# Splitting the last three even output tiles into latent and context parts, with the odd norm between them

## The reference, cut to what matters

```python
def second_block(...):
    for i in range(DEPTH):                      # i = 0 even, i = 1 odd
        h_lat = rms_norm_2(x_lat, norm_g[i]) * (1.0 + sc_l) + sh_l
        h_ctx = rms_norm_2(x_ctx, norm_g[i]) * (1.0 + sc_c) + sh_c
        y_lat, y_ctx = even_mixer(...) if i % 2 == 0 else odd_mixer(...)
        x_lat = x_lat + g_l * y_lat             # y = mixed @ w_out
        if update_ctx:                          # true for i = 0 alone
            x_ctx = x_ctx + g_c * y_ctx
    return rms_norm_2(x_lat, final_g)

def odd_mixer(h_lat, h_ctx, w_in, ...):
    cv, cgl, cg, dq, dk, dv, dg = split_cols(h_lat @ w_in, ODD_WIDTHS)
    oc = conformer_conv(cv, cgl, cg, dw_w, dw_b, ln_g, ln_b)   # 31 taps along the rows
```

## Time and profile before

| | us |
|---|---|
| median of three runs | 2627.19 (2627.0 to 2627.4) |
| the profiled execution: its own time | 2626.77 |
| its span, first to last instruction | 2625.00 |
| TensorE busy | 2535.7 (97%) |
| VectorE busy | 1646.6 (63%) |
| ScalarE busy | 1124.7 (43%) |
| mean granted TensorE clock | 0.992 |

### The profile page before, as it was taken

How to read it: one execution, slowest core, us unless ns; L and a number is a source line. 1 busy time by engine, 2 the same in 40 slices (tenths; PEclk the granted TensorE clock), 3 DMA queues, 4 the chain that set the end, 5 groups by cost and what they waited for, 6 DMA issues and landing times.

```text
span 2625.0 us, 34953 instructions
## 1 busy us (share of the span) xinstructions
PE 2535.7 (97%) x13470; PEld 2049.4 (78%) x13470; DVE 1646.6 (63%) x3123; ACT 1124.7 (43%) x2043; POOL 0.2 (0%) x4
## 2 busy tenths in 40 slices
PE   8999999999999999999999999999999999999998
PEld 6878888678888878788886788888876666888666
DVE  6766555455446776665653644478486677499764
ACT  4336443543222243464434422233345667232563
POOL 0000000000000000000000000000000000000000
PEclk9999999999999999999999999999999999999999
DMA  4220033123336522201331233375110000232311
GB/s 159 92 69 22 17 121 124 37 73 105 96 97 214 187 74 91 66 16 38 124 113 41 80 97 97 96 256 180 41 49 19 23 17 17 65 87 65 84 48 48
DMA packets 74083, 219.38 MB, mean 84 GB/s; under 512 B 21312, under 2 KB 21568, under 8 KB 73152
## 3 DMA queue, kind: packets, MB, share of 16 engines
q1 hardware_dynamic: 48384, 176.29, 20.7%
q10 hardware_dynamic: 25536, 40.87, 5.0%
HBM read 215.03 MB, written 2.10 MB: 83 GB/s over the span
## 4 chain that ended last, share of the span: by engine, by line
PE 87%; DVE 7%; ACT 3%; issue 2%; ACTq 0%; DVEq 0%
PE bank L579 21%; PE bank L580 21%; PE bank L581 21%; PE bank L832 4%; PE bank L796 3%; PE bank L806 3%; PE bank L1401 1%; DVE w_lo L545 1%; PE bank L1388 1%; PE bank L698 1%; PE bank L610 1%; PE bank L611 1%; PE bank L612 1%; DVE e_s L897 1%; ACT w_hi L538 1%
## 5 line engine op out<-in xcount | busy, mean ns | idle before, releaser
L579 PE MATMUL bank<-a_hi,w_hi 128*128 128x512 f32 (+1 forms) x1480 | 588.9, 398 | 19.8 <-DVE w_lo L545 14.4
L538 ACT ACTIVATE w_hi<-w_raw 128x1024 fp32r<-128x1024 f32 x334 | 353.0, 1060 | 570.0 <-PE bank L581 540.9
L581 PE MATMUL bank<-a_hi,w_lo 128*128 128x512 f32 (+1 forms) x1480 | 579.1, 391 | 0.0
L580 PE MATMUL bank<-a_lo,w_hi 128*128 128x512 f32 (+1 forms) x1480 | 578.5, 391 | 0.0
L545 DVE TENSOR_TENSOR w_lo<-w_raw,w_hi 128x1024 fp32r<-128x1024 f32 x334 | 407.6, 1223 | 250.0 <-ACT w_hi L538 249.1
L579 PEld LDWEIGHTS bank<-a_hi,w_hi 128*128 128x128 f32 (+1 forms) x1480 | 277.8, 188 | 88.8 <-issue 14.4
L581 PEld LDWEIGHTS bank<-a_hi,w_lo 128*128 128x128 f32 (+1 forms) x1480 | 277.5, 188 | 60.7
L580 PEld LDWEIGHTS bank<-a_lo,w_hi 128*128 128x128 f32 (+1 forms) x1480 | 278.1, 188 | 58.3 <-issue 1.4
L579 PE MATMUL bank<-b_hi,w_hi 128*128 128x512 f32 x704 | 257.1, 365 | 1.0 <-DVE w_lo L545 0.8
L580 PE MATMUL bank<-b_lo,w_hi 128*128 128x512 f32 x704 | 248.7, 353 | 0.0
L581 PE MATMUL bank<-b_hi,w_lo 128*128 128x512 f32 x704 | 247.4, 351 | 0.0
(11 more groups left out here) (392 smaller groups left out, 3955.3 us busy)
## 6 DMA issues: line engine op xcount, KB each, us to landing
w_raw<-w_tiles SPq DMA_DIRECT2D x334, 512.0 KB, 3.5
mod_raw<-mod_tiles ACTq DMA_DIRECT2D x48, 512.0 KB, 4.2
d_bias<-rpb_rows ACTq DMA_DIRECT2D x16, 224.0 KB, 4.3
hT<-xT ACTq DMA_DIRECT2D x8, 256.0 KB, 6.1
m_in<-memT ACTq DMA_DIRECT2D x2, 1024.0 KB, 4.7
mod_cond<-cond_rows ACTq DMA_DIRECT2D x2, 1024.0 KB, 5.4
out<-hT ACTq DMA_DIRECT2D x8, 256.0 KB, 2.2
ctx_sq<-ctxT ACTq DMA_DIRECT2D x1, 1024.0 KB, 9.1
```

The source lines that it names most:

```text
L538: act.activation(w_hi[:, t % SPLIT, :], w_raw[:, t % RAW, :], ACT.Copy).then_inc(sem("w_rounded"), 1)
L579: pe.matmul(o, wh, hi[:, k, :n], start=k == 0, stop=False)
L580: pe.matmul(o, wh, lo[:, k, :n], start=False, stop=False)
L581: mm = pe.matmul(o, wl, hi[:, k, :n], start=False, stop=k == kc - 1)
```

## The change

From even output tile T5 (`EVEN_SPLIT`) on, the products are made in two passes. TensorE first makes the latent parts of T5, T6 and T7, then the context parts of T5, T6 and T7; the latent sum of squares stands after chunk 6 of the context part of T5, the latent rows after chunk 2 of that of T6. The context sum moves behind the pair T8/T9, the context rows behind T10. The three filler groups of this seam (four matmuls) are gone. VectorE and ScalarE make the odd input from the latent stream while the context parts are still being multiplied, and take the remaining three context parts between the chunks. The weight buffers of T5 to T7 come free only with their context parts.

```diff
         def even_out_pe(pe):
             group_tiles_pe(pe, [(0, 0), (0, 1)], both("e_y"), inputs_ready(("e_mix",)))
-            for c in range(2, KC):
+            for c in range(2, EVEN_SPLIT):
                 product(pe, (0, c), both("e_y"))
+            first = blocks[0] // KC
+            lat, ctx_part = both("e_y")
+            for c in range(EVEN_SPLIT, KC):
+                for _ in part_steps(pe, first + c - EVEN_SPLIT, (0, c), lat):
+                    pass
+            for c in range(EVEN_SPLIT, KC):
+                for k, _ in enumerate(part_steps(pe, first + c - EVEN_SPLIT, (0, c), ctx_part, last=True)):
+                    if c == EVEN_SPLIT and k == KC - 2:
+                        ssq_pe(pe, ("m2", 1, "lat"), S)
+                    if c == EVEN_SPLIT + 1 and k == 2:
+                        rstd_pe(pe, ("m2", 1, "lat"), S)
+        EVEN_SPLIT = KC - SPLIT
+        def part_steps(pe, t, key, part, last=False):
+            name, hi, lo, n = part
+            o = claim(pe, name, *key, hold=True)[:, :n]
+            pe.wait_ge(sem("w_split"), t + 1)
+            for k in range(KC):
+                wh, wl = head(w_hi[:, t % SPLIT, :], k), head(w_lo[:, t % SPLIT, :], k)
+                pe.matmul(o, wh, hi[:, k, :n], start=k == 0, stop=False)
+                pe.matmul(o, wh, lo[:, k, :n], start=False, stop=False)
+                mm = pe.matmul(o, wl, hi[:, k, :n], start=False, stop=k == KC - 1)
...
+                yield
...
+        def odd_begin_dve(dve):
+            lat = PARTS[0]
+            even_out_take_dve(dve, "ctx", EVEN_SPLIT)
+            lo_after(dve, "e_y/lat", 0, EVEN_SPLIT)
             for c in range(KC):
+                mod_scaled_dve(dve, 1, lat, c)
                 if c:
+                    mod_low_dve(dve, 1, lat, c - 1)
+                if c == 1:
+                    even_out_take_dve(dve, "ctx", EVEN_SPLIT + 1)
+                    lo_after(dve, "e_y/lat", 0, EVEN_SPLIT + 1)
+                if c == 2:
+                    odd_ctx_sum_dve(dve, EVEN_SPLIT)
+                if c == 4:
+                    even_out_take_dve(dve, "ctx", KC - 1)
+                    odd_ctx_sum_dve(dve, EVEN_SPLIT + 1)
+            mod_low_dve(dve, 1, lat, KC - 1)
+            odd_ctx_sum_dve(dve, KC - 1)
+            lo_after(dve, "e_y/lat", 0, KC - 1)
...
         def odd_in_pe(pe):
             group_pe(pe, [((1,), both(name)[0]) for name, *_ in OJ[:2]], mod_ready(1, "lat"))
             for i, (name, _, _, with_ctx) in enumerate(OJ):
                 if name[:2] not in LATE and i >= 2:
                     product(...)
+                if i == 1:
+                    ctx_ssq_pe(pe, 1)
+                if i == 2:
+                    ctx_rstd_pe(pe, 1)
...
             even_out_pe(pe)
-            warm_pe(pe, 2, "m2", 1)
-            ssq_pe(pe, ("m2", 1, "lat"), S)
-            ctx_ssq_pe(pe, 1)
-            warm_pe(pe, 1, "m2_rstd", 1)
-            rstd_pe(pe, ("m2", 1, "lat"), S)
-            ctx_rstd_pe(pe, 1)
-            warm_pe(pe, 1, "odd_in")
             odd_in_pe(pe)
...
             even_out_dve(dve)
-            inverse_dve(dve, ("m2", 1, "lat"), S)
+            odd_begin_dve(dve)
             ctx_inverse_dve(dve, 1)
-            lo_after(dve, "e_y/lat", 0, KC - 1)
-            mod_chunks_dve(dve, 1, PARTS[0])
             mod_chunks_dve(dve, 1, PARTS[1], 0, 2)
             for name, *_ in OJ[:2]:
                 lo_after(dve, f"{name}/lat", 1)
             mod_chunks_dve(dve, 1, PARTS[1], 2)
```

More of the change, by code:

```diff
@@ L1865, in mod_chunks_dve, with mod_scaled_dve, mod_low_dve @@
         def mod_chunks_dve(dve, i, part, first=0, last=KC):
-            p, _, sl, n, w = part
-            t = mod_tmp(i)
-            row = bank(dve, "rstd", "m2", i, p)
             for c in range(first, last + 1):
                 if c < last:
[L1872 to L1878, removed]
-                if c > first:
[L1880 to L1884, removed]
+                    mod_scaled_dve(dve, i, part, c)
+                if c > first:
+                    mod_low_dve(dve, i, part, c - 1)
+        def mod_scaled_dve(dve, i, part, c):
+            p, _, sl, n, w = part
+            row = bank(dve, "rstd", "m2", i, p)
+            if c >= 2:
+                dve.wait_ge(*when("shifted_in", i, p, c - 2))
+            dve.scalar_tensor_tensor(out=mod_tmp(i)[:, c % 2, sl], in0=stream(p)[:, c, :n],
+                                     scalar=mod_gain[:, w, c:c + 1], in1=row[:, :n], op0=ALU.mult, op1=ALU.mult)\
+               .then_inc(*(freed("rstd", "m2", i, p, also=("scaled", i, p, c)) if c == KC - 1
+                           else done("scaled", i, p, c)))
+        def mod_low_dve(dve, i, part, c):
+            p, _, sl, n, w = part
+            dve.wait_ge(*when("hi", i, p, c))
+            dve.scalar_tensor_tensor(out=b_lo[:, c, sl], in0=mod_tmp(i)[:, c % 2, sl], scalar=mod[:, i, c, w:w + 1],
+                                     in1=b_hi[:, c, sl].bitcast(f32), op0=ALU.add, op1=ALU.subtract)\
+               .then_inc(*done("shifted_in", i, p, c))
         def both(name):
@@ L2137, in even_out_pe @@
             group_tiles_pe(pe, [(0, 0), (0, 1)], both("e_y"), inputs_ready(("e_mix",)))
-            for c in range(2, KC):
+            for c in range(2, EVEN_SPLIT):
                 product(pe, (0, c), both("e_y"))
-        def even_out_dve(dve):
-            for c in range(KC):
[L2144 to L2151, removed]
-                if c:
-                    odd_sum_dve(dve, c - 1)
-            odd_sum_dve(dve, KC - 1)
@@ L2162, in odd_squares_act, with odd_square_act @@
+        def odd_square_act(act, p, c):
+            act.wait_ge(*when("h2", p, c))
+            if p == "lat":
                 if c >= 2:
@@ L2164, in odd_squares_act @@
                 act.activation(sq[:, c % 2, :], hT[:, c, :], ACT.Square).then_inc(*done("sq", "m2", 1, "lat", c))
-                act.wait_ge(*when("h2", "ctx", c))
+            else:
                 if c >= 2:
```

58 lines of the change are left out of this document (48 added, 10 removed).

## The result

| | before | changed |
|---|---|---|
| median of 20 timed runs each, us | 2627.29 (2623.34 to 2631.68) | 2630.07 (2627.49 to 2632.6) |
| the profiled execution: its own time | 2626.77 | 2629.22 |
| its span | 2625.0 | 2627.4 |
| TensorE busy | 2535.7 | 2534.5 |
| mean granted clock | 0.992 | 0.990 |

The forecast was 2629.0. The chain that ended last has the same shares as in the earlier trace rows, TensorE 87%.

What follows compares the result with a forecast made beforehand. TensorE holds 87% of the chain, but VectorE's first tap decides: T10 comes 6.15 us sooner, yet late context rows put the tap 1.84 later. 2626.77 + 1.84 = 2628.6, on the median 2629.0; range 2625.8 to 2632.3.

Steps and rivals of the forecast that it cites:

- The quantity that decides: VectorE never pauses from first tap to softmax, so the first tap's shift, +1.84 us, goes through to the end.
- Even output, sum and rows: At T5 to T7: latent sum meets TensorE without a wait; even output ends and pair starts near 2288.3, 7.3 us earlier.
- The pair: T8/T9: TensorE waits of 0.2, 0.7, then 0.1 each; end at 2300.3, T10 at 2300.75, 6.15 us ahead.
- R and the wait of VectorE: Context rows readable at 2306.9, VectorE idle from about 2301.6; first tap R + 12.65 = 2319.55, 1.84 us later.
- TensorE's two waits: 4.1 us before T11, 4.3 before T13, shrinking to 1.3 with half clock; no cost beyond the 1.84.
- T11 then takes up to 3.0 us more: Half clock expected behind the 4.1 us wait; T12 ends at 2324.7 and the loss falls into the second wait.
- Rival B: Full clock through T11's wait, half clock in T13: T16 4.1 us later, end 2631.3, or 2633.8; chance 0.12.
- They no longer cover anything: The seam's four fillers, about 3.8 us, go because the wait they stood in is gone.
- Moved DMAs: Loads of T11 to T13 hang on splits of T8 to T10, wanted seven or more us later; no cost.
- buffers (D): Bank or weight buffer held until the context parts, delaying the pair 3 us or more: 2632; chance 0.08.
- an early R (C): Context rows sooner through VectorE gaps or a shorter chain: shift -1.5 to +0.8, 2626 to 2628; chance 0.18.
- the gain arriving (A): VectorE slack before T13, or context rows before T10 ends, keeps the seam's 5.7 us: 2621.5; chance 0.06.

Runs made afterwards that it cites:

- early: Changed kernel with last context take and sums sooner, context rows inside T10, T11/T12 splits ahead of context chunks; ratio 0.9991, timed again 0.9989.
- splits first: Changed kernel with the splits of T11 and T12 ahead of the context chunks on VectorE and ScalarE; ratio 1.0005.
- the second comparison of the changed kernel: Changed kernel unaltered, profiled and timed again against the kernel before; ratio 1.0017, +4.5 us (2.1 to 6.8).
- without fillers: Kernel before with only its four filler matmuls at the seam taken out; ratio 1.0013.
- rows moved: Kernel before with only the context sum put behind the pair T8/T9 and the context rows behind T10; ratio 1.0034.
- fillers in the waits: Changed kernel with four filler matmuls behind the context rows and three ahead of T13; ratio 1.0014.
- inside T10: Changed kernel with the context rows behind chunk 1 of T10 in place of behind all of T10; ratio 0.9999.
- still later: Changed kernel with four filler matmuls in front of the context rows, behind T10; ratio 1.0023.

## Why the prediction was right, step by step

**The quantity that decides.** The prediction said that VectorE's first tap decides and that its shift goes through. In thirteen profiles softmax moved with the first tap to within 0.2 us, over a range of 12.7 us (52.90 to 65.61). For the end of the program one correction is needed. From T16 to the attention TensorE takes 91.80 to 91.85 us in all thirteen, and the timed differences go with that start: every interval in the table holds the shift of the attention column, those of early and of splits first included. The timing alone could hardly tell the two columns apart, since only the second comparison of the changed kernel leaves out the tap's shift (1.89, interval from 2.1); it is the profiles that show the difference. From the tap to T16 lie 24.57 or 24.58 us where T13 runs at full clock (the kernel before twice, without fillers, rows moved, and fillers in the waits), 25.0 to 25.2 where some 3 us of T13 run at half clock, and 26.28 where nearly 6 do. So T13's clock is part of the price: 0.45 us in the changed kernel.

**Even output, sum and rows.** Forecast pair start 2288.3, measured 2287.08 + 0.98 = 2288.06 on the clock of before. The sum does meet TensorE without a wait.

**The pair.** Forecast waits of 0.2, 0.7 and some 0.1, measured one of 0.38; end forecast 2300.3, measured 2300.24; T10 2300.75 against 2300.60.

**R and the wait of VectorE.** Forecast 2306.9 behind an idle time of 5.3 us; measured 2306.77 and 5.54. First tap forecast +1.84, measured +1.88, +1.89 and +1.86. This term carries the forecast, and the experiments that moved only the rows (inside T10, still later, moved alone) show that it is the cause and not a companion.

**TensorE's two waits.** In front of T11 4.1 forecast, 3.81 measured. In front of T13 1.3 forecast, 2.78 measured: the step "T11 then takes up to 3.0 us more" took the 6.0 us stretch of the earlier trace rows for the half clock; it lasted about 3 us and lost half as much. In the second profile there was none, and the wait was 4.40, near the 4.3 that the prediction has for full clock. That the first drop is paid out of the second wait was right; the 6.8 us of half clock in the kernel with only the rows moved cost nothing at T16 either. T16 was forecast 1.84 us later and came 2.33 later: the step that no drop costs anything beyond the tap's shift holds for T11, not for T13.

**Rival B** happened in its mechanism: T13 begins at half clock in all three profiles of the changed kernel (its first matmul takes 0.77 us for 0.47), in the second one exactly as the rival had it, with full clock in T11. Its price was wrong. It assumed 6 us of half clock (3.0 lost, 0.7 regained, T16 +4.1); about 3 us came, T16 moved by 2.33, and of that only 0.45 is the clock's. The argument that kept its chance low, that the longer waits were the ones followed by half clock, does not fit the prediction's own rows: 2.18 us was followed by it, 2.28 was not.

**The fillers.** "They no longer cover anything" holds for the changed kernel. What the prediction had no term for is what they did before: 3.6 us at the first tap (56.54 to 60.13). It cost the forecast nothing, since the context matmuls took over; as the prediction did not reckon with that, this was luck. Whoever takes fillers out without putting work there pays it.

**Moved DMAs, buffers (D), an early R (C), the gain arriving (A).** The pair waits only 0.38 us, for `b_lo` and not for a buffer. VectorE did stand at the rows. The gain was at the seam and did not arrive.

**Small slips.** The terms for the last latent part add up to 2280.13, not 2280.25, and T16's first matmul stands at 2341.51 in the trace of before, not at 2341.41. Neither bears on the sum.

**The size.** Predicted +1.8, timed +3.4 (1.8 to 5.0), so the forecast lies at the near end of the interval. T13's clock accounts for 0.45. For the rest there is one candidate with rows. Behind the attention's start TensorE waits 2.28 us for `rstd` in every profile, about 74 us in. In some executions half clock follows, in others not. Here the two profiles of the early kernel, the same code, first and second:

```profile
2501.63 2.10 PE L797 MATMUL bank<-d_k,d_q 64*128 64x512 f32 x8 [2.28 <-ACT rstd L2424]
2503.66 0.79 PE L579 MATMUL bank<-b_hi,w_hi 128*128 128x512 f32 x1
```

```profile
2505.11 1.56 PE L797 MATMUL bank<-d_k,d_q 64*128 64x512 f32 x8 [2.28 <-ACT rstd L2424]
2506.60 0.50 PE L579 MATMUL bank<-b_hi,w_hi 128*128 128x512 f32 x1
```

The mean rest of the program is 192.9 us in the seven profiles with that drop and 191.5 in the six without. The drop was in one of four profiles of the kernels with whole tiles, and in six of nine of those with split tiles; the changed kernel had it in two of three, the early one in one of two. So it is not a fixed property of a kernel. Whether a kernel's phase shifts the odds (6 of 9 against 1 of 4, times 1.4 us, would be 0.6 of the missing 1.1), these few profiles can't settle; it stays open. The spread of single executions is too large for it: the code ahead of the take is the same in both kernels, yet the take lies at 2258.91 to 2262.81 in the three profiles of the changed one. A fixed cost of the split tiles elsewhere does not show: the early kernel has them too, and its timed -2.4 and -2.9 match its attention start, 3.0 sooner, though within intervals of about 2.4 to either side.

## What to carry to other kernels

Before closing a gap of the busiest engine, find the engine that hands it work afterwards and ask which of its instructions the moved work feeds: here two small matmuls, moved behind three products on TensorE, cost VectorE 9 us, more than the closed gap gave. In a queue that runs in order, put what waits for a late result behind what could run, and the producer of that result as early as its input allows. Take fillers out only where useful work comes into their place, and see from the granted clock that it does.

## What the runs showed of the hardware

- Half clock behind identical waits is not the same from one execution to the next. Behind 3.81 us of waiting the changed kernel had some 3 us of it in one profile and none in another; with only the rows moved it was 6.8 us behind the same 3.81; behind 2.28 us, seven of thirteen profiles had some 3 us. In front of T13 the eight profiles with a wait of 2.55 to 5.72 us all had it; the five with 0.82 or 1.74 us, or with fillers in the wait, did not.
- A wait of 2.42 us without fillers left TensorE at 1.2 GHz for more than 12 us, through tiny matmuls and a second wait of 2.18 us. Matmuls of one column suffer as well: eight took 1.87 us for 1.05.
- VectorE never passed a blocked instruction: the splits of T11 and T12, queued behind the context chunk, waited wherever the code has them behind it, and ran 4.8 us ahead of it (2300.30 and 2305.06) in the kernel that puts them first. The Trainium skill (TensorE: Matmul & The Clock Gate, Architectural detail) has the elementwise engines strictly in order; the rows agree.
